# One accumulator in HBM for all routed blocks of a mixture-of-experts step: chained scatters, skipped filler rows, asserted registers

## The chip, the core and the metric

The kernel runs on one core of a Trainium2 chip. The metric is the device time of one launch in microseconds (us), as the median of several executions. Engines are called as in the profile: PE is TensorE (PEld its weight loads), DVE VectorE, ACT ScalarE, POOL GpSimd, SP SyncE. SP issues most loads and stores, POOL the indirect ones.

## The reference

One layer of a hybrid backbone on 1152 tokens (1024 + 128) of width 1024: a mixer, a residual with layer norm, a mixture of experts and a last residual with layer norm. The change lies in the mixture and in the last norm:

```python
scores = jax.nn.sigmoid((x @ p["w_router"]).astype(jnp.float32))
...
y = (jax.nn.silu(xb @ p["w_exp_gate"][e]) * (xb @ p["w_exp_up"][e])) @ p["w_exp_down"][e]
y_assign = y_blocks.reshape(-1, d)[dest] * w_sorted[:, None]
routed = jax.ops.segment_sum(y_assign, tok, num_segments=t).astype(x.dtype)
shared = (jax.nn.silu(x @ p["w_sh_gate"]) * (x @ p["w_sh_up"])) @ p["w_sh_down"]
return (routed + shared).reshape(bsz, n, d)
...
x = layer_norm(DEEPNORM_ALPHA * x + g2 * moe(h, p), p["ln2_g"], p["ln2_b"])
```

Each token goes to 8 of 64 experts, so there are 1152 x 8 = 9216 assignments. An expert's tokens are cut into blocks of 128, and the last block of an expert is filled up with filler rows.

## The kernel before

The kernel works in three phases; the change touches the third (`phase3_*`), which each engine writes out as its own program, with semaphores between them.

**Tokens and blocks.** Tokens are nine tiles of 128. The shared expert runs on them as blocks b = 0 to 8, the routed blocks follow as b = 9 + j. The number of routed blocks is known only at run time. `routed_steps` therefore loops over pairs of blocks with branches on a loaded register, and each engine reads the numbers it needs (the block count, the expert of block j, whether block j starts a new expert) with `entry`, a load of a table entry into a register (line 440).

**A step.** In step s the engines do, each in its own order:
- PE: gate and up products of block s, transpose of h of block s-1, transpose of the gathered rows of block s+2 (line 911), down product of block s-2 (lines 856 for all products).
- ACT: silu of s, high parts of h and x, the high part of a new expert's gate and up weights (line 653), the scaled copy of y of block s-2 from PSUM into one of two buffers `yb` (line 734), the high part of new down weights (line 658).
- DVE: the gate product of s, low parts, the index column of the gather (line 1157), the low part of new gate and up weights (line 987), the index column of the scatter of block s-2 (line 1162).
- POOL: the gather of block s+4 (line 614), the low part of new down weights (line 595, a 4.6 us operation), then the scatter of block s-2 (line 623).
- SP: the weight loads, 3 MB for each expert, into two buffers each, every load behind the landing of an earlier one and the splitting of the one whose buffer it takes (lines 469 to 501).

**Accumulation.** There are two accumulators in HBM, `acc_dram[0]` and `acc_dram[1]`, one for each parity p of a block. The scatter of block j is an indirect DMA that adds its 128 rows of `yb[p]` to `acc_dram[p]`. It waits for the landing of the scatter of block j-2, which is the earlier one into the same accumulator and the same buffer; the ACT copy and the DVE index copy wait for the same landing. Filler rows carry token numbers from T on and land in 128 rows behind the tokens (`NTRASH`). The shared expert's output is written plainly into `acc_dram[0]` (line 726), and `acc_dram[1]` is filled with zeros by POOL in phase 3's first lines (578 and 580), 5 MB. The gather already drops filler rows (`bounds_check=T - 1`), the scatter doesn't.

**Last stage.** When the last scatter has landed SP loads, for every tile, both accumulators and x1 (lines 563 to 566; three tiles of x1 are there already). DVE adds the two parts of tile 0 (line 1254), PE adds them for tiles 1 to 8 by products with the identity into PSUM (line 974), and DVE does the rest: times g2 (1258), plus x1 (1260), mean (1075) and normalization (1262, 1266), with ACT's square and root between.

Of the kernel before, what the change touches and what calls it, by code (L numbers as in the profile page):

```python
# [6 lines left out]
F32 = mybir.dt.float32  # L7
# [8 lines left out]
P = 128  # L16
D = 1024
# [18 lines left out]
NTRASH = P  # L36
# [78 lines left out]
def build(nc, A, out_prompt, out_sample, out_state, stage=9, dbg=None):  # L115

    ctx = ExitStack()
    with ctx:
# [9 lines left out]
        acc_dram = [nc.dram_tensor(f"acc{p}_dram", [T + NTRASH, D], F32).ap() for p in range(2)]  # L128
# [240 lines left out]
        def table(w, dtype=F32, parts=P):  # L369
# [26 lines left out]
        acc_t, acc1_t = carve(R01, GU_AT, NT, D), carve(R01, GU_AT + (NT + 1) * D, NT, D)  # L396
# [9 lines left out]
        (sel_ready, rank_mm, nb_ready, end_mm, cmp_ready, blk_mm, tables_ready, dest_ready, empty_out) = (sem(n) for n in (  # L406
             "sel_ready", "rank_mm", "nb_ready", "end_mm", "cmp_ready", "blk_mm", "tables_ready", "dest_ready",
             "empty_out"))
# [3 lines left out]
        gidx_ready, sidx_ready, sum_mm, sum_used = (sem(n) for n in ("gidx_ready", "sidx_ready", "sum_mm", "sum_used"))  # L412
# [25 lines left out]
        def entry(eng, place, min_val, max_val):  # L438

            return nc.values_load(place, engines=(eng.engine,), min_val=min_val, max_val=max_val,  # L440
                                  skip_runtime_bounds_check_because="block counts and expert numbers are bounded by the shapes")
# [18 lines left out]
        def landed_before(j, p):  # L460

            return 8 * (j - (p + 1) % 2) + 16

# [17 lines left out]
        def phase3_sync(sp):  # L481
# [21 lines left out]
            for i in range(NT + 2):  # L503
# [9 lines left out]
                if i == 2:  # L513
                    sp.wait_ge(setup_in, STATE_OUT)
                    for p in range(2):
                        sp.wait_ge(y_out[p], 16)
                    sp.wait_ge(empty_out, 16)
                    load_gate_up(sp, 0, A["w_sh_gate"][0], A["w_sh_up"][0])
                    load_down(sp, 0, A["w_sh_down"][0])
# [42 lines left out]
            for i in range(NT):  # L562
                sp.dma_start(acc_t[:, i, :], acc_dram[0][tile(i), :]).then_inc(fin_in[i], 16)
                sp.dma_start(acc1_t[:, i, :], acc_dram[1][tile(i), :]).then_inc(fin_in[i], 16)
                if i >= XE:
                    sp.dma_start(x1_t[i], x1_dram[tile(i), :]).then_inc(fin_in[i], 16)
# [7 lines left out]
        def phase3_pool(pool):  # L574
            tt = pool.tensor_tensor

            zero = S[:, SR].rearrange("p a b -> p (a b)")
            pool.dma_start(acc_dram[0][T:T + NTRASH].rearrange("p (h x) -> p h x", h=2),
                           zero.unsqueeze(1).to_broadcast((P, 2, 512))).then_inc(y_out[0], 16)
            pool.dma_start(acc_dram[1].rearrange("(p a) (h x) -> p (a h) x", p=P, h=2),  # L580
                           zero.unsqueeze(1).to_broadcast((P, 2 * (T + NTRASH) // P, 512))).then_inc(y_out[1], 16)
            pool.wait_ge(empty_out, 16)
# [34 lines left out]
            def scatter(b, p, j):  # L617

                pool.wait_ge(y_ready, b + 1)
                pool.wait_ge(sidx_ready, j + 1)  # L620
                pool.wait_ge(y_out[p], landed_before(j, p))
                pool.sem_inc(dma_turns)
                pool.indirect_dma_start(out=acc_dram[p], out_offset=bass.IndirectOffsetOnAxis(  # L623
                    ap=sidx[:, p:p + 1], axis=0), in_=yb[:, p, :], in_offset=None, compute_op=ALU.add).then_inc(y_out[p], 16)
# [20 lines left out]
        def phase3_act(act):  # L645
# [73 lines left out]
            def shared_out(b, p):  # L719
# [6 lines left out]
                act.dma_start(acc_dram[0][tile(b), :], yb[:, p, :]).then_inc(ysh_out[p], 16)  # L726
# [74 lines left out]
        def phase3_pe(pe, project):  # L801
# [165 lines left out]

            for i in range(1, NT):
                pe.wait_ge(fin_in[i], 48 if i < ST else 64)
                if i >= 3:  # L970
                    pe.wait_ge(sum_used, i - 1)
                for h in range(2):
                    for n, part in enumerate((acc_t, acc1_t)):
                        last = mm(ps[:, 2 * (i % 2) + h, :], ident, part[:, i, h * 512:(h + 1) * 512], start=(n == 0), stop=(n == 1))
                last.then_inc(sum_mm, 1)

        def phase3_dve(dve, done):
# [268 lines left out]
            for s in range(NT + 1):  # L1246
                i = s
                if i < NT:
                    x, y = acc_t[:, i, :], acc1_t[:, i, :]
                    k = 2 * NT + i  # L1250
                    r = k % 2
                    if i == 0:
                        dve.wait_ge(fin_in[0], 48)
                        done(tt(x, x, y, ALU.add))
                    else:
                        dve.wait_ge(sum_mm, i)
                    total = two(x) if i == 0 else ps[:, 2 * (i % 2):2 * (i % 2) + 2, :]
                    tt(two(x), total, two(g2_row[cond_of(i)]), ALU.mult).then_inc(sum_used, 1)
# [5 lines left out]
                if i >= 0:  # L1264
                    scale = ln_scale(2 * NT + i)
                    stt(acc_t[:, i, :], acc1_t[:, i, :], scale, ln2_row[:, 1, :], ALU.mult, ALU.add).then_inc(fin_ready, 1)
# [57 lines left out]
        def _(pool):  # L1324
# [40 lines left out]
            for r in range(2):  # L1365
                for d in range(2):
# [8 lines left out]
            pool.dma_start(list_dram.rearrange("(q c r) w -> q c (r w)", q=117, r=P),  # L1375
                           C["emptylist"][0:117].unsqueeze(1).to_broadcast((117, NE * T // P // 117, 2 * P))).then_inc(empty_out, 16)
# [812 lines left out]
```

## Time and profile before

| what | value |
|---|---|
| device time, median of 3 executions | 1862.57 us (1859.29, 1862.57, 1863.57) |
| profiled execution: span from first to last instruction | 1837.1 us |
| device time over the span, taken from the median | 25.5 us |
| PE busy, share of the span | 1708.8 us, 93% |
| mean granted TensorE clock | 0.965 |
| DMA | 102447 packets, 406.50 MB |
| first gather to landing of the last scatter, about | 709 to 1774 us |

The profiled execution's own time is its span of 1837.1 us with what lies before the first and behind the last instruction; only the span is on the page, and the median stands 25.5 us above it. Shares of busy time are averages over very different stages: what a change of the routed stage is worth has to be read in that stage.

### The profile page before, as it was taken

What the parts mean: (1) busy time and instruction counts of PE and PEld (TensorE: products, weight loads), DVE (VectorE), ACT (ScalarE), POOL (GpSimd) and SP (SyncE); (2) the same over time, 40 slices, a digit from 0 to 9 for tenths busy, and PEclk for the clock granted to TensorE, in tenths of its full rate; (3) what the DMA queues carried; (4) which work ended last, traced back from release to release, by engine and by line L of the source; (5) the groups of instructions that cost most, each with busy time, mean ns of one, the idle gap of its engine ahead of it and who ended that gap; (6) DMA issues with size and microseconds to landing.
All of it is one profiled execution on the core that took longest, in us unless ns stands there. A gap on an engine that the chain in (4) does not pass through costs nothing.

```text
span 1837.1 us, 30736 instructions
## 1 busy us (share of the span) xinstructions
PE 1708.8 (93%) x8570; PEld 1334.1 (73%) x8571; DVE 927.2 (50%) x1442; ACT 840.2 (46%) x950; POOL 759.4 (41%) x445
## 2 busy tenths in 40 slices
PE   6999999999999898999999989999999989999845
PEld 2677788888455686888877878888888768888621
DVE  7432210167578873654554455335645645456429
ACT  2320011341033433765666566445666666567612
POOL 3230000400003562665465566634774565546630
PEclk9999999999999898999999999999999999999868
DMA  8515531022542453898799899768998999889786
GB/s 347 183 50 178 169 108 33 19 93 81 194 182 89 144 182 147 281 336 267 223 303 303 256 308 351 222 180 240 328 316 234 298 303 319 237 271 319 241 257 255
DMA packets 102447, 406.50 MB, mean 221 GB/s; under 512 B 17820, under 2 KB 34457, under 8 KB 74624
## 3 DMA queue, kind: packets, MB, share of 16 engines
q1 hardware_dynamic: 62576, 289.25, 42.3%
q0 software_dynamic: 37232, 107.16, 24.0%
q10 hardware_dynamic: 2592, 9.44, 1.7%
q8 instruction: 32, 0.52, 0.1%
q14 instruction: 15, 0.12, 0.0%
HBM read 339.94 MB, written 84.72 MB: 231 GB/s over the span
## 4 chain that ended last, share of the span: by engine, by line
PE 66%; DMA 15%; DVE 8%; ACT 4%; issue 4%; POOL 2%; ACTq 1%; SPq 1%; POOLq 0%; DVEq 0%
PE ps L856 35%; PE ps L2001 12%; DMA raw<-w_exp_up 6%; DMA arena<-hx_dram,arena 5%; PE ps L911 4%; PE ps L2142 4%; PE ps L1924 2%; DMA acc_dram<-arena 2%; PE ps L2132 1%; POOL d_split L595 1%; PE ps L888 1%; PE ps L1974 1%; PE ps L2097 1%; ACT d_split L658 1%; PE ps L2036 1%
## 5 line engine op out<-in xcount | busy, mean ns | idle before, releaser
L856 PE MATMUL ps<-gu_split,xT 128*128 (+1 forms) x2712 | 637.7, 391 | 0.2 <-issue 0.2
L856 PEld LDWEIGHTS ps<-gu_split,xT 128*128 128x128 f32 x2712 | 511.3, 189 | 107.7 <-issue 0.9
L856 PE MATMUL ps<-d_split,hTe 128*128 (+1 forms) x1356 | 357.6, 415 | 34.7 <-ACT arena L734 34.6
L595 POOL TENSOR_TENSOR d_split<-raw,d_split (+1 forms) x65 | 299.5, 4608 | 194.3 <-ACT d_split L658 193.9
L987 DVE TENSOR_TENSOR gu_split<-raw,gu_split (+1 forms) x130 | 293.3, 2297 | 127.3 <-ACT gu_split L653 127.3
L856 PEld LDWEIGHTS ps<-d_split,hTe 128*128 128x128 f32 x1356 | 259.1, 197 | 90.2 <-issue 38.3
L653 ACT ACTIVATE gu_split<-raw (+1 forms) x130 | 241.2, 1907 | 62.7 <-SPq L497 61.0
L614 POOL DMA_INDIRECT arena<-hx_dram,arena x108 | 140.7, 1303 | 189.4 <-DVE arena L1157 157.5
L1151 DVE TENSOR_TENSOR arena<-ps,arena 128x256 f32<-128x256 f32 x113 | 70.5, 624 | 288.1 <-ACT arena L740 288.0
L623 POOL DMA_INDIRECT acc_dram<-arena x104 | 167.1, 1607 | 90.2 <-DVE arena L1162 60.6
L1141 DVE TENSOR_TENSOR xT<-ps,xT 128x1024 fp32r<-128x1024 f32 x115 | 140.7, 1224 | 101.0 <-ACT xT L712 101.0
L2001 PE MATMUL ps<-hT_split,w_split 128*128 128x512 f32 (+1 forms) x816 | 189.9, 390 | 0.0
L2001 PEld LDWEIGHTS ps<-hT_split,w_split 128*128 128x128 f32 x816 | 150.2, 188 | 37.1 <-issue 7.1
L734 ACT ACTIVATE arena<-ps,arena 128x1024 f32<-128x1024 f32 x104 | 115.3, 1109 | 114.4 <-PE ps L856 57.4
L712 ACT ACTIVATE xT<-ps 128x1024 fp32r<-128x1024 f32 x115 | 118.1, 1027 | 65.6 <-PE ps L911 65.2
L911 PE MATMUL ps<-const,arena 128*128 128x128 f32 x920 | 123.2, 278 | 23.0 <-DMA arena<-hx_dram,arena 15.0
L740 ACT ACTIVATE arena<-ps 128x256 f32<-128x256 f32 x113 | 43.0, 380 | 216.0 <-PE ps L856 215.9
L589 POOL DMA_INDIRECT list_dram<-arena x72 | 79.3, 1101 | 144.6 <-DVE arena L1064 123.6
L2142 PE MATMUL ps<-arena 128*128 128x512 f32 x288 | 129.6, 605 | 1.4 <-DVE arena L1092 0.8
L658 ACT ACTIVATE d_split<-raw (+1 forms) x65 | 124.1, 1909 | 7.0 <-SPq L501 4.9
L911 PEld LDWEIGHTS ps<-const,arena 128*128 128x128 f32 x920 | 106.3, 143 | 25.4 <-issue 10.0
L2142 PEld LDWEIGHTS ps<-arena 128*128 128x128 f32 x288 | 54.6, 194 | 65.2 <-issue 62.8
(284 smaller groups left out, 1433.0 us busy)
## 6 DMA issues: line engine op xcount, KB each, us to landing
raw<-w_exp_gate SPq DMA_DIRECT2D x64, 1024.0 KB
raw<-w_exp_up SPq DMA_DIRECT2D x64, 1024.0 KB
raw<-w_exp_down SPq DMA_DIRECT2D x64, 1024.0 KB
arena<-w_ada SPq DMA_DIRECT2D x16, 1024.0 KB, 4.9
arena<-x_dram SPq DMA_DIRECT2D x18, 512.0 KB, 10.7
arena<-acc_dram SPq DMA_DIRECT2D x18, 512.0 KB, 11.3
arena<-ada_halves SPq DMA_DIRECT2D x4, 2048.0 KB, 24.3
w_raw<-w_in SPq DMA_DIRECT2D x16, 512.0 KB, 4.8
```

What stands on the lines that cost most here:

```text
L595: tt(d_split(q, 1), raw_d(q), d_split(q, 0).bitcast(F32), ALU.subtract).then_inc(d_low, 1)
L614: pool.indirect_dma_start(out=xg[:, p, :], out_offset=None, in_=hx_dram, in_offset=bass.IndirectOffsetOnAxis(ap=gidx[:, p:p + 1], axis=0), ...
L623: pool.indirect_dma_start(out=acc_dram[p], out_offset=bass.IndirectOffsetOnAxis(ap=sidx[:, p:p + 1], axis=0), in_=yb[:, p, :], in_offset=N ...
L653: a(gu_split(q, 0, half * (GU // 2), GU // 2), raw_gu(q, half), ACT.Copy).then_inc(gu_high, 1)
L658: a(d_split(q, 0), raw_d(q), ACT.Copy).then_inc(d_high, 1)
L712: a(xT[:, p, 0, :].rearrange("p (h x) -> p h x", h=2), ps[:, 0:2, :], ACT.Copy).then_inc(xT_high, 1)
L856: last = mm(dst, lhs(a, j), rhs(b, j), start=(t == 0), stop=(t == len(terms) - 1))
L911: last = pe.transpose(ps[:, c // 4, (c % 4) * P:(c % 4 + 1) * P], xg[:, p, c * P:(c + 1) * P], ident)
L987: last = tt(part(1), raw_gu(q, half), part(0).bitcast(F32), ALU.subtract)
L1141: tt(two(xT[:, p, 1, :]), ps[:, 0:2, :], two(xT[:, p, 0, :].bitcast(F32)), ALU.subtract).then_inc(xT_ready, 1)
L2001: last = mm(dst, lhsT, rhs, start=(t == 0), stop=(t == len(terms) - 1))
L2142: last = mm(ps[:, 2 * (i % 2) + h, :], yT[:, j, tile(i)], w_out[:, j, h * 512:(h + 1) * 512], start=(start and j == chunks[0]), stop=(j == 1))
```

## The change

- One accumulator `acc_dram` of exactly T rows in place of two of T + 128. Nothing is filled with zeros any more, since the shared expert's plain writes cover all rows.
- The scatter of block j waits for the landing of the scatter of block j-1 (`other_landed`). ACT's and DVE's waits on the landing of block j-2 stay.
- The scatter gets `bounds_check=T - 1, oob_is_err=False`: filler rows are skipped.
- The last stage loads one accumulator for each tile. The sums of line 974 on PE and of line 1254 on DVE are gone, and DVE multiplies from SBUF.
- `entry` no longer skips the bounds check of the loaded value: behind each load stands an assertion.
- The list tensor in HBM is initialized by two DMAs in place of one, and these now bring the semaphores `y_out` to 16, in place of the two fills.

```diff
-        acc_dram = [nc.dram_tensor(f"acc{p}_dram", [T + NTRASH, D], F32).ap() for p in range(2)]
+        acc_dram = nc.dram_tensor("acc_dram", [T, D], F32).ap()
...
-            return nc.values_load(place, engines=(eng.engine,), min_val=min_val, max_val=max_val,
-                                  skip_runtime_bounds_check_because="block counts and expert numbers are bounded by the shapes")
+            return nc.values_load(place, engines=(eng.engine,), min_val=min_val, max_val=max_val)
...
+        def other_landed(j, p):
+
+            return 8 * j + 16 if p else 8 * j + 24
...
-                sp.dma_start(acc_t[:, i, :], acc_dram[0][tile(i), :]).then_inc(fin_in[i], 16)
-                sp.dma_start(acc1_t[:, i, :], acc_dram[1][tile(i), :]).then_inc(fin_in[i], 16)
+                sp.dma_start(acc_t[:, i, :], acc_dram[tile(i), :]).then_inc(fin_in[i], 16)
...
-            zero = S[:, SR].rearrange("p a b -> p (a b)")
-            pool.dma_start(acc_dram[0][T:T + NTRASH].rearrange("p (h x) -> p h x", h=2),
-                           zero.unsqueeze(1).to_broadcast((P, 2, 512))).then_inc(y_out[0], 16)
-            pool.dma_start(acc_dram[1].rearrange("(p a) (h x) -> p (a h) x", p=P, h=2),
-                           zero.unsqueeze(1).to_broadcast((P, 2 * (T + NTRASH) // P, 512))).then_inc(y_out[1], 16)
-            pool.wait_ge(empty_out, 16)
+            for p in range(2):
+                pool.wait_ge(y_out[p], 16)
...
-                pool.wait_ge(y_out[p], landed_before(j, p))
+                pool.wait_ge(y_out[1 - p], other_landed(j, p))
                 pool.sem_inc(dma_turns)
-                pool.indirect_dma_start(out=acc_dram[p], out_offset=bass.IndirectOffsetOnAxis(
-                    ap=sidx[:, p:p + 1], axis=0), in_=yb[:, p, :], in_offset=None, compute_op=ALU.add).then_inc(y_out[p], 16)
+                pool.indirect_dma_start(out=acc_dram, out_offset=bass.IndirectOffsetOnAxis(
+                    ap=sidx[:, p:p + 1], axis=0), in_=yb[:, p, :], in_offset=None, bounds_check=T - 1, oob_is_err=False,
+                    compute_op=ALU.add).then_inc(y_out[p], 16)
...
-            for i in range(1, NT):
-                pe.wait_ge(fin_in[i], 48 if i < ST else 64)
-                if i >= 3:
-                    pe.wait_ge(sum_used, i - 1)
-                for h in range(2):
-                    for n, part in enumerate((acc_t, acc1_t)):
-                        last = mm(ps[:, 2 * (i % 2) + h, :], ident, part[:, i, h * 512:(h + 1) * 512], start=(n == 0), stop=(n == 1))
-                last.then_inc(sum_mm, 1)
...
-                    if i == 0:
-                        dve.wait_ge(fin_in[0], 48)
-                        done(tt(x, x, y, ALU.add))
-                    else:
-                        dve.wait_ge(sum_mm, i)
-                    total = two(x) if i == 0 else ps[:, 2 * (i % 2):2 * (i % 2) + 2, :]
-                    tt(two(x), total, two(g2_row[cond_of(i)]), ALU.mult).then_inc(sum_used, 1)
+                    dve.wait_ge(fin_in[i], 32 if i < ST else 48)
+                    tt(x, x, g2_row[cond_of(i)], ALU.mult).then_inc(sum_used, 1)
...
-            pool.dma_start(list_dram.rearrange("(q c r) w -> q c (r w)", q=117, r=P),
-                           C["emptylist"][0:117].unsqueeze(1).to_broadcast((117, NE * T // P // 117, 2 * P))).then_inc(empty_out, 16)
+            lists = list_dram.rearrange("(q c r) w -> q c (r w)", q=117, r=P)
+            for p, (c0, c1) in enumerate(((0, 2), (2, NE * T // P // 117))):
+                pool.dma_start(lists[:, c0:c1], C["emptylist"][0:117].unsqueeze(1).to_broadcast((117, c1 - c0, 2 * P))).then_inc(y_out[p], 16)
```

Two places as they stand in the built programs. First POOL's queue in the loop over pairs, the scatter of an even j and the gather of the next block; before:

```order
L620 REGISTER_ALU [waits y_ready]
L621 ISA [waits sidx_ready]
L623 DMA acc_dram<-arena 1280x1024 [waits y_out1]
L611 REGISTER_ALU
L612 REGISTER_ALU [waits gidx_ready]
L614 DMA arena<-hx_dram,arena 128x1024 [waits x_t]
L440 ISA
L440 TENSOR_LOAD arena
L478 COMPARE_AND_BRANCH
```

and with the change (line 618 is the scatter, 609 the gather, 438 the load of a table entry):

```order
L615 REGISTER_ALU [waits y_ready]
L616 ISA [waits sidx_ready]
L618 DMA acc_dram<-arena 1152x1024 [waits y_out0]
L606 REGISTER_ALU
L607 REGISTER_ALU [waits gidx_ready]
L609 DMA arena<-hx_dram,arena 128x1024 [waits x_t]
L438 ISA
L438 TENSOR_LOAD arena
L438 ISA x2
L479 COMPARE_AND_BRANCH
```

The order is the same. The scatter of an even block waits on the other semaphore, and the next gather stands behind it as before. Behind the load stand two more instructions, of which one only computes a register and the other is the assertion.

Second the first tiles of the last stage on DVE; before (line 1254 is the sum of tile 0, 1258 the product with g2):

```order
L1254 TENSOR_TENSOR arena<-arena 128x1024 [waits fin_in0,row_ready]
L1258 TENSOR_TENSOR arena<-arena 128x1024 [waits dve_step]
L1260 SCALAR_TENSOR_TENSOR arena,small<-arena 128x1024 [waits sum_used]
L1075 TENSOR_SCALAR small<-small 128x1 [waits dve_step]
L1262 SCALAR_TENSOR_TENSOR arena<-arena,small 128x1024 [waits mean_ready]
L1258 TENSOR_TENSOR arena<-ps,arena 128x1024 [waits sum_mm,dve_step]
```

and with the change (line 1240 is the product):

```order
L1240 TENSOR_TENSOR arena<-arena 128x1024 [waits fin_in0,row_ready]
L1242 SCALAR_TENSOR_TENSOR arena,small<-arena 128x1024 [waits sum_used]
L1062 TENSOR_SCALAR small<-small 128x1 [waits dve_step]
L1244 SCALAR_TENSOR_TENSOR arena<-arena,small 128x1024 [waits mean_ready]
L1240 TENSOR_TENSOR arena<-arena 128x1024 [waits fin_in1,dve_step]
```

The sum of tile 0 is gone, and tile 1 waits for its own load in place of PE's sum.

## Rows read from the trace of the kernel before

**Rows 1.** The page's head: busy us (share of the span) x instructions.

```profile
span 1837.1 us, 30736 instructions
PE 1708.8 (93%) x8570; PEld 1334.1 (73%) x8571; DVE 927.2 (50%) x1442; ACT 840.2 (46%) x950; POOL 759.4 (41%) x445
```

**Rows 2.** Stretches of the routed stage: length, engines' busy us, clock, DMA share, GB/s.

```profile
1110.00:1290.00 180.00, 180.00 (x894) 151.16 (x894) 81.16 (x115) 96.39 (x103) 90.42 (x47) 1.00 0.82 245
...
1290.00:1370.00 80.00, 77.64 (x385) 64.94 (x384) 42.62 (x53) 52.15 (x50) 57.00 (x23) 1.00 0.96 331
1450.00:1520.00 70.00, 59.03 (x266) 48.17 (x265) 35.94 (x41) 44.59 (x41) 42.48 (x18) 0.93 0.95 306
1690.00:1770.00 80.00, 59.33 (x248) 47.12 (x246) 29.64 (x37) 41.58 (x38) 46.55 (x21) 0.86 0.82 241
```

**Rows 3.** Who waited for whom: us in total, times, longest.

```profile
PE ps L856 <- ACT arena L734: 34.6, 12, 6.3
PE ps L911 <- DMA arena<-hx_dram,arena: 15.0, 8, 7.1
...
ACT arena L734 <- DMA acc_dram<-arena: 57.0, 22, 6.3
```

**Rows 4.** The scatter's line: ns of its issue on POOL min/median/max; its landing.

```profile
L623 POOL DMA_INDIRECT acc_dram<-arena x104: 1557/1589/3474, 761.4 to 1767.8; - x104
...
DMA to landing us min/median/max: 5.8/10.8/13.5
```

**Rows 5.** DMA queue of POOL: packets, MB, share of 16 engines' span.

```profile
q0 software_dynamic: 37232, 107.16, 24.0%
```

**Rows 6.** POOL in order of time, 1331 to 1356: start us, us, what [idle before].

```profile
1332.81 1.59 POOL L623 DMA_INDIRECT acc_dram<-arena  x1 [0.16 <-issue]
1334.71 1.03 POOL L614 DMA_INDIRECT arena<-hx_dram,arena  x1 [0.31 <-issue]
...
1340.57 1.59 POOL L623 DMA_INDIRECT acc_dram<-arena  x1 [0.17 <-issue]
1342.46 2.32 POOL L614 DMA_INDIRECT arena<-hx_dram,arena  x1 [0.30 <-issue]
```

**Rows 7.** PE in order of time, 1343 to 1360: the transposes of gathered rows.

```profile
1348.13 1.09 PE L911 MATMUL ps<-const,arena 128*128 128x128 f32 x8 [1.52 <-DMA arena<-hx_dram,arena]
...
1357.51 1.04 PE L911 MATMUL ps<-const,arena 128*128 128x128 f32 x8
```

**Rows 8.** POOL in order of time, 1744 to 1775: the last three scatters.

```profile
1756.85 1.59 POOL L623 DMA_INDIRECT acc_dram<-arena  x1 [0.17 <-issue]
1761.84 1.56 POOL L623 DMA_INDIRECT acc_dram<-arena  x1 [3.40 <-ACT arena L734]
1767.83 1.56 POOL L623 DMA_INDIRECT acc_dram<-arena  x1 [4.43 <-ACT arena L734]
```

**Rows 9.** The chain that ended last, 1747 to 1774: start us, us, what.

```profile
1747.69 11.91 DMA acc_dram<-arena
...
1767.83 6.13 DMA acc_dram<-arena
1774.13 0.32 SPq L563
```

**Rows 10.** DVE in order of time, 1774 to 1791: the first tiles of the last stage.

```profile
1779.10 1.23 DVE L1254 TENSOR_TENSOR arena<-arena 128x1024 f32<-128x1024 f32 x1 [13.65 <-DMA arena<-acc_dram]
...
1783.07 1.28 DVE L1262 SCALAR_TENSOR_TENSOR arena<-arena,small 128x1024 f32<-128x1024 f32 x1
1789.12 1.23 DVE L1258 TENSOR_TENSOR arena<-ps,arena 128x1024 f32<-128x1024 f32 x1 [4.77 <-PE ps L974]
```

**Rows 11.** Line 563, the loads of the first accumulator: issue to landing.

```profile
DMA to landing us min/median/max: 3.7/10.9/15.6
```

**Rows 12.** Line 440, a register operation beside PE's table loads, ns min/median/max.

```profile
L440 PEldq FUSED_REGOPS  x206: 46/46/57, 741.3 to 1751.2; - x103
```

**Rows 13.** Who POOL waited for: us in total, times, longest.

```profile
POOL list_dram L589 <- DVE arena L1064: 123.6, 3, 108.3
```

More of the change, by code:

```diff
@@ L35 @@
 PAIRS = (NB + 1) // 2
-NTRASH = P
 GU = 2 * D * FF // P
@@ L395, in build @@
         ln2_row = carve(R0, 6 * D, 2, D)
-        acc_t, acc1_t = carve(R01, GU_AT, NT, D), carve(R01, GU_AT + (NT + 1) * D, NT, D)
+        acc_t, norm_t = carve(R01, GU_AT, NT, D), carve(R01, GU_AT + (NT + 1) * D, NT, D)
         g2_row = [carve(R0, 8 * D, D), carve(R01, GU_AT + NT * D, D)]
@@ L405, in build @@
         x0r_in, x1_out, h2_out = (x0r_in0, x0r_in1), (x1_out0, x1_out1), (h2_out0, h2_out1)
-        (sel_ready, rank_mm, nb_ready, end_mm, cmp_ready, blk_mm, tables_ready, dest_ready, empty_out) = (sem(n) for n in (
-             "sel_ready", "rank_mm", "nb_ready", "end_mm", "cmp_ready", "blk_mm", "tables_ready", "dest_ready",
-             "empty_out"))
+        (sel_ready, rank_mm, nb_ready, end_mm, cmp_ready, blk_mm, tables_ready, dest_ready) = (sem(n) for n in (
+             "sel_ready", "rank_mm", "nb_ready", "end_mm", "cmp_ready", "blk_mm", "tables_ready", "dest_ready"))
         list_out, logit_out, list_row_ready, list_in, list_t, lists_ready = (sem(n) for n in (
@@ L411, in build @@
         mean_ready, sq_ready, std_ready = sem("mean_ready"), sem("sq_ready"), sem("std_ready")
-        gidx_ready, sidx_ready, sum_mm, sum_used = (sem(n) for n in ("gidx_ready", "sidx_ready", "sum_mm", "sum_used"))
+        gidx_ready, sidx_ready, sum_used = (sem(n) for n in ("gidx_ready", "sidx_ready", "sum_used"))
         dma_turns = sem("dma_turns")
@@ L516, in phase3_sync @@
                         sp.wait_ge(y_out[p], 16)
-                    sp.wait_ge(empty_out, 16)
                     load_gate_up(sp, 0, A["w_sh_gate"][0], A["w_sh_up"][0])
@@ L725, in shared_out @@
                 act.wait_ge(y_ready, b + 1)
-                act.dma_start(acc_dram[0][tile(b), :], yb[:, p, :]).then_inc(ysh_out[p], 16)
+                act.dma_start(acc_dram[tile(b), :], yb[:, p, :]).then_inc(ysh_out[p], 16)
             def routed_out(b, p, j):
@@ L1248, in phase3_dve @@
                 if i < NT:
-                    x, y = acc_t[:, i, :], acc1_t[:, i, :]
+                    x, y = acc_t[:, i, :], norm_t[:, i, :]
                     k = 2 * NT + i
                     r = k % 2
-                    if i == 0:
-                        dve.wait_ge(fin_in[0], 48)
-                        done(tt(x, x, y, ALU.add))
-                    else:
-                        dve.wait_ge(sum_mm, i)
-                    total = two(x) if i == 0 else ps[:, 2 * (i % 2):2 * (i % 2) + 2, :]
-                    tt(two(x), total, two(g2_row[cond_of(i)]), ALU.mult).then_inc(sum_used, 1)
+                    dve.wait_ge(fin_in[i], 32 if i < ST else 48)
+                    tt(x, x, g2_row[cond_of(i)], ALU.mult).then_inc(sum_used, 1)
                     dve.wait_ge(sum_used, i + 1)
@@ L1265, in phase3_dve @@
                     scale = ln_scale(2 * NT + i)
-                    stt(acc_t[:, i, :], acc1_t[:, i, :], scale, ln2_row[:, 1, :], ALU.mult, ALU.add).then_inc(fin_ready, 1)
+                    stt(acc_t[:, i, :], norm_t[:, i, :], scale, ln2_row[:, 1, :], ALU.mult, ALU.add).then_inc(fin_ready, 1)
         @block.sync
```

## The prediction, as written before the changed kernel ran

> **What bounds the kernel now.** I began with the page's head: PE is busy in 93% of a span of 1837.1 us [rows 1], so whatever leaves PE's program full costs nothing. The reader should see that this is an average. I then cut the routed stage, 1110 to 1770, into stretches [rows 2]. From 1110 to 1290 PE is busy in all 180 us, at full clock, with the DMA engines at 0.82: that stretch is bound by PE's instructions. In the three others shown PE is idle for 2.4, 11.0 and 20.7 us, 34 us in all, with DMA shares of 0.96, 0.95 and 0.82. These are the places where experts with a single block follow each other, so that every step needs another 3 MB of weights. Third I read who waited for whom [rows 3]: PE's products wait 34.6 us for ACT's copy of y, its transposes 15.0 us for gathers, and ACT's copy waits 57.0 us for landings of scatters, mostly without PE noticing. Fourth the scatter itself [rows 4]: 104 of them in 1006 us, one every 9.8 us, and a landing of 10.8 us in the median, 5.8 at least. That is the danger of this change: a chain of scatters, each behind the landing of the last, would need 10.8 us for each block if the median held, and there are 9.8.
>
> **The change part by part.** The sum is made against the profiled execution, whose time I take as 25.5 us above its span, which is the median of 1862.57 us.
>
> *The last stage* is the surest part. DVE starts at 1779.10, when both parts of tile 0 have landed, adds them, ends tile 0's work at 1784.35 and then stands for 4.77 us until PE has summed tile 1 [rows 10]. From 1789.12 on it works without a gap, and keeps doing so. With one accumulator tile 0 needs only its first load, issued at 1774.13 [rows 9] and landed 3.7 us later in the best case [rows 11]: start at 1777.9, 1.2 us earlier. The sum of tile 0 goes, 1.25 us from start to start. The wait of 4.77 us goes as well, since tile 1 needs only its own load, the next in the queue, and DVE has some 4 us of work on tile 0. Together -7.2 us. The product with g2 costs the same from SBUF as from PSUM: the two additions and products shown all take 1.23 us. What is late next is DVE itself, over nine tiles. Ends of the range: -5 us if the load takes a median-like time, -8 if it is as fast as it can be.
>
> *The drain* in front of it gets longer. The last four scatters are issued at 1747.69, 1756.85, 1761.84 and 1767.83; the first lands after 11.91 us, at 1759.60, the last, alone on the queue, after 6.13 us [rows 8, 9]. Chained, with 6.1 us for each and 0.2 us from a landing to the next issue: the second is issued at 1759.8 and lands at 1765.9, the third 1766.1 and 1772.2, the fourth 1772.4 and 1778.5, where it was 1773.96. That is +4.5 us; with the least landing of 5.8 us [rows 4] +3.6, with the median for one of them +9. I take +4.5, as 6.13 is the row of a lone scatter in this very place. The Trainium skill (DMA: Bandwidth & Descriptors, section Anatomy of one DMA) fits such a transfer as about 2.0 us plus bytes over 436 GB/s. That gives some 3.2 us for the 512 KB here, the chain would then be ready before the fourth block is, the drain would cost nothing and the sum would be 4.5 us lower. The trace has no scatter under 5.8 us, so the measurement decides.
>
> *The chain in the middle.* Where scatters are far apart, the one ahead has landed. Where two are 5 to 8 us apart, the second now waits. But they share one queue: the second also landed late before, up to 13.5 us after its issue [rows 4], as its rows stood behind those of the first. Its landing hardly moves, and ACT's and DVE's waits are for landings. POOL waits in the second scatter, and behind it stand only the next gather and the next low part. I take 0 for the waits: POOL is busy for 41% of the span [rows 1] and has idle time in front of most gathers. Bounds: nothing, and 20 us (second rival).
>
> *The skipped rows.* Of 104 x 128 = 13312 rows 9216 are assignments, 4096 (31%) filler. POOL's queue moves 107.16 MB in 24.0% of the span of all engines [rows 5]; the scatters carry 54.5 MB of it. By bytes that is half, 224 us, 2.2 us of all sixteen engines for one scatter. So 31% is 69 us of transfer time, but in PE-bound stretches nobody waits for it. It can only pay in the 34 us of idle time. Ends: 0 and -34. I take -2, near the lower end, for two reasons. The largest loss, 20.7 us of 80, is where the DMA share is lowest, 0.82 [rows 2]: a chain of single waits (load, split on ACT, DVE and POOL, next load), not the mean traffic. And filler rows are always the tail of a block. A load ends with its slowest engine, and rows taken from the tail relieve it only if the rows of a scatter are dealt to the engines in turn. The Trainium skill (same page, section The descriptor swizzle) says that they are not: partitions 0 to 63 belong to engines 0 to 7, so a block of 40 to 64 tokens leaves eight engines empty and gives the others all their eight rows. By it the relief is near 0; with rows dealt evenly it would be ten times what I take (first rival). No row here separates the engines.
>
> *The assertions.* Each table load gets two more register instructions behind it. The nearest row is a fused register operation of 46 ns, 206 of them on PE [rows 12], so 2 x 206 x 0.046 = 19 us of PE's sequencer. In the 180 us without a gap the loads of both blocks of each step are already hidden behind queued matmuls, and 0.1 us each stays hidden too. I take 0 (ends: 0 and +19).
>
> *The fills and the list.* The 5 MB of zeros went out long before they were needed: POOL stands 123.6 us in front of its list scatters, waiting for DVE [rows 13]. If that cover were gone, two issues on POOL would count, about 2 us. The list's second DMA is hidden by the same wait. Nine loads fewer on SP are in the last stage's term. All 0.
>
> **Sum:** -7.2 + 4.5 - 2 = -4.7 us, so 1857.9 us.
>
> **Rivals.**
> 1. *The skip relieves the loads.* If rows are dealt evenly, about 21 blocks in the three stretches lose a third to a half of 2.2 us, 14 to 23 us; I price it at 20. For it: shares of 0.95 and 0.96 with PE idle [rows 2]. Against it: what stands above. Time: 1862.6 - 2.7 - 20 = 1839.9.
> 2. *The gather behind the waiting scatter* (slower). Scatters at 1332.81 and 1340.57, a gather at 1342.46 [rows 6]. With a landing of 11.4 us the second now waits until 1344.2, 3.7 us, and pushes that gather to 1346.2. The gather ahead of it, issued at 1334.71, held PE up for 1.52 us at 1348.13, so it took 13.3 us; the next is needed at 1357.51 [rows 7]. From 1346.2 that makes 1359.5: PE stands 2.0 us. There are ten places with scatters some 7.8 us apart, so +20 us, 1877.9. It decides where a delay is over the gather's slack, here 1.7 us. Against it: the gather's 13.3 us held its time behind the scatter's rows in the queue, which now have left earlier.
> 3. *The assertions show* on PE or ACT: up to +19 us, 1877.
> 4. *The skip skips nothing* that costs, because the filler rows' descriptors are still made and moved: the sum loses its 2 us, 1859.9. The gather has the same check and takes 1.03 us on POOL where the scatter takes 1.59 [rows 6], which speaks against more cost there.
>
> **How the numbers follow.** My forecast has 0.54, rivals 1 to 4 have 0.16, 0.14, 0.07 and 0.09. About 0.2% of the time, 3.7 us, is what a measurement of this kernel can tell from no change. Faster by more than that means under 1858.8: a little over half of the forecast (its own range is 1853 to 1864, from the ends of the first two terms and a few us of relief or stall), and all of rival 1, 0.48. Within 0.2%: a third of the forecast, most of rival 4, some of 2 and 3, 0.29. Slower: the rest, 0.23. The range from 1841 to 1871 takes in the forecast, rival 4, half of rival 1 and the milder forms of rivals 2 and 3.
>
> **What would show it.** Right: line 974 is gone, DVE goes from tile 0 to tile 1 without a gap and the stretch from SP's first load to the end is some 56 us long, not 63; the last scatter is issued at the landing of the third, about 6 us before SP's first load; POOL's queue has 4096 packets and 17 MB less; PE is still busy in the whole of a stretch of multi-block experts. Wrong: a sum of PE waits for gathers clearly over 15.0 us (rival 2), a DMA share that falls in the bad stretches together with PE's idle time (rival 1), gaps on PE or ACT behind table loads (rival 3), an unchanged packet count (rival 4).

## The result, and the profile of the changed kernel

| | before | changed |
|---|---|---|
| device time, median | 1863.07 us (4 executions) | 1901.58 us (1893.56 to 1906.46, 4 executions) |
| ratio of the times, 95% interval | | 1.021 (1.0183 to 1.0237) |
| profiled execution: span | 1837.1 us | 1891.8 us |

The changed kernel is slower by 38.5 us. I had forecast 1857.9 us, in a range that ended at 1871, so the forecast is wrong in sign and in size.

First, from the changed kernel's page, the head and the queue of POOL; under them who waited for whom (us in total, times, longest). They answer to [rows 1, 3, 5]:

```profile
span 1891.8 us, 32015 instructions
PE 1689.9 (89%) x8506; PEld 1322.7 (70%) x8507; DVE 930.9 (49%) x1441; ACT 845.2 (45%) x950; POOL 776.8 (41%) x444
...
q0 software_dynamic: 35808, 84.65, 18.8%
```

```profile
POOL acc_dram L618 <- DMA acc_dram<-arena: 212.9, 43, 8.9
...
ACT arena L730 <- DMA acc_dram<-arena: 90.1, 30, 7.1
...
PE ps L907 <- DMA arena<-hx_dram,arena: 34.2, 17, 8.0
...
PE ps L852 <- ACT arena L730: 32.1, 11, 7.0
```

The queue has lost 22.5 MB: 16.7 MB of filler rows and 5.8 MB of fills. It has lost only 1424 packets, and all of them before the routed stage; why the filler rows' 4096 packets are still there is shown below. PE's idle time hasn't fallen but grown. Its products still wait as long for ACT's copies as before, 32.1 us, but its transposes now wait 34.2 us for gathers, where they waited 15.0 [rows 3]. POOL has a wait that it never had: 212.9 us for landings of scatters, in 43 places. My second rival describes both.

Now one place in order of time, POOL and then PE (start us, us, line, and in brackets the idle time ahead and what ended it):

```profile
1128.66 3.22 POOL L618 DMA_INDIRECT acc_dram<-arena  x1 [2.59 <-DMA acc_dram<-arena]
1132.19 1.05 POOL L609 DMA_INDIRECT arena<-hx_dram,arena  x1 [0.30 <-issue]
...
1138.55 2.96 POOL L618 DMA_INDIRECT acc_dram<-arena  x1 [0.64 <-issue]
1141.82 1.37 POOL L609 DMA_INDIRECT arena<-hx_dram,arena  x1 [0.31 <-issue]
1150.15 1.60 POOL L618 DMA_INDIRECT acc_dram<-arena  x1 [6.97 <-DVE arena L1149]
1152.06 1.04 POOL L609 DMA_INDIRECT arena<-hx_dram,arena  x1 [0.30 <-issue]
```

```profile
1150.82 0.38 PE L884 MATMUL ps<-const,arena 128*128 128x128 f32 x2
1153.08 1.09 PE L907 MATMUL ps<-const,arena 128*128 128x128 f32 x8 [1.88 <-DMA arena<-hx_dram,arena]
```

The gathers leave right behind the scatters, at 1132.19, 1141.82 and 1152.06: 9.6 and 10.2 us apart, and PE's step is 9.3. PE's transposes at 1153.08 need the gather of 1141.82, which left behind the scatter of 1138.55 and took 10.7 us; by then POOL had already stood 2.59 us for the landing that the scatter of 1128.66 waited for. PE stands for 1.88 us, and the delay stays. The scatter of 1138.55 lands at 1149.2; the next may not leave before, and goes at 1150.15. The row puts POOL's idle 6.97 us down to DVE's index copy of 1149.3, but that copy is the next scatter's, and had waited for the same landing.

The chain of work that ended last shows the pace. Its longest pieces between 1093 and 1120 (start us, us, what) are landings in a row:

```profile
1093.62 10.90 DMA acc_dram<-arena
...
1105.56 10.54 DMA acc_dram<-arena
...
1118.43 9.36 DMA acc_dram<-arena
```

From scatter to scatter it takes 11.9 and 12.9 us here, against the step of 9.3. Of the whole span's chain 12% are landings of scatters, where it was 2%. Where PE isn't late it loses nothing. From 1180 to 1340 it is busy all the time, as in [rows 2]:

```profile
1180.00:1340.00 160.00, 160.00 (x792) 134.33 (x792) 66.93 (x97) 85.58 (x89) 79.25 (x40) 1.00 0.71 208
```

The loss comes in jumps of 1 to 6 us where single-block experts bring weight loads beside the scatters, and little of it is made good.

The drain and the last stage answer to [rows 8 to 11]. The chain that ended last, then DVE in order of time, then the accumulator's loads:

```profile
1804.71 10.76 DMA acc_dram<-arena
...
1816.34 5.84 DMA acc_dram<-arena
...
1823.05 5.95 DMA acc_dram<-arena
...
1829.83 6.22 DMA acc_dram<-arena
...
1836.22 3.49 DMA arena<-acc_dram
```

```profile
1839.80 1.22 DVE L1240 TENSOR_TENSOR arena<-arena 128x1024 f32<-128x1024 f32 x1 [17.33 <-DMA arena<-acc_dram]
...
1842.52 1.28 DVE L1244 SCALAR_TENSOR_TENSOR arena<-arena,small 128x1024 f32<-128x1024 f32 x1
1843.83 1.22 DVE L1240 TENSOR_TENSOR arena<-arena 128x1024 f32<-128x1024 f32 x1
```

The last four scatters go one behind the other, 11.6, 6.7 and 6.8 us apart. From SP's first load to the end it is 1891.8 - 1836.2 = 55.6 us, where it was 63.0, and DVE goes from tile 0 to tile 1 without a gap.

**The two spans can't be subtracted.** The changed kernel's profiled execution took 1893.56 us by its own clock, 1.8 over its span. By the same 1.8 the profiled execution of before took 1838.9, which is 20 us under the fastest of its timed ones. Aligned by PE's shared-expert and routed steps, the two traces are level (within 0.5 us) until 655 us and 22.2 us apart at the first routed step, before any routed scatter. The time goes at two places, 660 to 670 and 685 to 700, where the profile shows nothing that PE waits for and its matmuls still come one by one, as here:

```profile
661.74 0.19 PE L810 MATMUL ps<-arena 128*128 128x64 bf16 x1 [1.24 <-issue]
663.14 0.21 PE L810 MATMUL ps<-arena 128*128 128x64 bf16 x1 [1.21 <-issue]
665.23 0.21 PE L810 MATMUL ps<-arena 128*128 128x64 bf16 x1 [1.89 <-issue]
667.34 0.21 PE L810 MATMUL ps<-arena 128*128 128x64 bf16 x1 [1.89 <-issue]
```

Whether the change brought this was one of the questions for the runs.

### The profile page after: what moved, and what is told of

It reads as the page before. It is cut to its first block, busy times and chain, and to the rows that moved or that the text cites. A ratio compares the mean times of both kernels' runs of the same rounds, so it can differ in the third digit from the quotient of the medians.

```text
span 1891.8 us, 32015 instructions
## 1 busy us (share of the span) xinstructions
PE 1689.9 (89%) x8506; PEld 1322.7 (70%) x8507; DVE 930.9 (49%) x1441; ACT 845.2 (45%) x950; POOL 776.8 (41%) x444
## 4 chain that ended last, share of the span: by engine, by line
PE 55%; DMA 19%; DVE 8%; issue 7%; POOL 4%; ACT 4%; POOLq 1%; ACTq 1%; SPq 0%; DVEq 0%
PE ps L852 27%; DMA acc_dram<-arena 12%; PE ps L1984 11%; DMA arena<-hx_dram,arena 4%; PE ps L2125 4%; PE ps L907 3%; POOL d_split L590 3%; DMA raw<-w_exp_up 3%; PE ps L1907 2%; PE ps L2115 1%; PE ps L1957 1%; ACT gu_split L649 1%; ACT d_split L654 1%; PE ps L884 1%; PE ps L2019 1%
## 5 line engine op out<-in xcount | busy, mean ns | idle before, releaser
L852 PE MATMUL ps<-d_split,hTe 128*128 (+1 forms) x1356 | 358.2, 415 | 38.0 <-ACT arena L730 32.1
L974 DVE TENSOR_TENSOR gu_split<-raw,gu_split (+1 forms) x130 | 297.3, 2328 | 142.2 <-ACT gu_split L649 141.1
L618 POOL DMA_INDIRECT acc_dram<-arena x104 | 190.1, 1828 | 310.6 <-DMA acc_dram<-arena 212.9
L609 POOL DMA_INDIRECT arena<-hx_dram,arena x108 | 135.7, 1257 | 87.7 <-DVE arena L1144 52.6
L907 PE MATMUL ps<-const,arena 128*128 128x128 f32 x920 | 126.1, 282 | 42.2 <-DMA arena<-hx_dram,arena 34.2
L736 ACT ACTIVATE arena<-ps 128x256 f32<-128x256 f32 x113 | 42.9, 380 | 190.4 <-PE ps L852 184.6
L2125 PEld LDWEIGHTS ps<-arena 128*128 128x128 f32 x288 | 53.5, 190 | 65.4 <-issue 61.2
```

The costliest lines, as they stand in the source:

```text
L609: pool.indirect_dma_start(out=xg[:, p, :], out_offset=None, in_=hx_dram, in_offset=bass.IndirectOffsetOnAxis(ap=gidx[:, p:p + 1], axis=0), ...
L618: pool.indirect_dma_start(out=acc_dram, out_offset=bass.IndirectOffsetOnAxis(ap=sidx[:, p:p + 1], axis=0), in_=yb[:, p, :], in_offset=None ...
L852: last = mm(dst, lhs(a, j), rhs(b, j), start=(t == 0), stop=(t == len(terms) - 1))
L907: last = pe.transpose(ps[:, c // 4, (c % 4) * P:(c % 4 + 1) * P], xg[:, p, c * P:(c + 1) * P], ident)
L974: last = tt(part(1), raw_gu(q, half), part(0).bitcast(F32), ALU.subtract)
L2125: last = mm(ps[:, 2 * (i % 2) + h, :], yT[:, j, tile(i)], w_out[:, j, h * 512:(h + 1) * 512], start=(start and j == chunks[0]), stop=(j == 1))
```

## The experiments

Ratios are to the kernel before, timed beside each run on the same chip, with their 95% intervals. 0.001 is 1.9 us. In free_empty and wait_empty a part of the computation is left out.

| run | accumulators | wait | skip | registers | median us | ratio |
|---|---|---|---|---|---|---|
| assert_only | 2 | no | no | asserted | 1865.8 | 1.0028 (1.0011 to 1.0046) |
| clamp_two | 2 | no | no | clamped | 1859.4 | 0.9991 (0.9975 to 1.0007) |
| skip_two_acc | 2 | no | yes | asserted | 1861.0 | 1.0003 (0.9984 to 1.0022) |
| wait_two_acc | 2 | yes | no | asserted | 1912.0 | 1.0258 (1.0217 to 1.0299) |
| wait_half | 2 | every second | no | asserted | 1890.8 | 1.0176 (1.0146 to 1.0206) |
| one_acc_no_skip | 1 | yes | no | asserted | 1906.0 | 1.0248 (1.0222 to 1.0274) |
| clamp_one_acc | 1 | yes | yes | clamped | 1892.3 | 1.0184 (1.0156 to 1.0212) |
| gather_first | 1 | yes, a step later | yes | asserted | 1962.6 | 1.0552 (1.0523 to 1.0582) |
| free_empty | 2 | no | all rows | asserted | 1831.9 | 0.9856 (0.9830 to 0.9883) |
| wait_empty | 2 | yes | all rows | asserted | 1834.2 | 0.9863 (0.9838 to 0.9888) |
| clamp_skip_two | 2 | no | yes | clamped | 1855.3 | 0.9973 (0.9957 to 0.9988) |
| lean_two | 2 | no | yes | clamped | 1856.0 | 0.9981 (0.9963 to 1.0000) |

**The parts alone.** In assert_only only the reason that let the assertions be left out is taken from the kernel before:

```diff
-            return nc.values_load(place, ..., skip_runtime_bounds_check_because="...")
+            return nc.values_load(place, engines=(eng.engine,), min_val=min_val, max_val=max_val)
```

> The kernel before with the assertions of the loaded registers alone; two accumulators, no new wait, no skip. Theory W (the loss is the wait of a scatter for the landing of the one ahead, with the gathers behind it on POOL): the PE step is 9.3 us and its sequencer runs ahead, so the assertions show at most in the unprotected stretches: 1860 to 1868. Theory A (the loss is the assertions: two register operations and a check, about 0.2 us at each load of the expert tables on every engine): 1890 to 1905, with PE idle behind the table loads. Theory C (part of the loss, up to 22 us, is the two places between 660 and 700 us where PE's matmuls come 1.2 to 1.9 us apart with nothing to wait for, which the new code brought): only a profile that has them here would blame the assertions' code.

Measured: +5 us by the ratio (2 to 9). The median, 1865.8, lies in the range of theory W and far from that of theory A. In clamp_two one register operation takes the place of each assertion:

```diff
...
+            with eng.register() as r:
+                eng.reg_alu(r, v, min_val, mybir.AluOpType.max)
+                return eng.snap(r, min_val=min_val, max_val=max_val)
```

> The kernel before, where each loaded register is held above its least value by one register operation instead of the two and the check of an assertion; nothing else. Theory W: within 4 us of the kernel before, 1860 to 1866. Theory A: a third to a half of the loss, 1873 to 1885. Theory C: no slow matmuls at 660 to 700 us if the kernel before has none either; if they are here too, they belong to every kernel's executions and explain nothing of the difference.

Measured: level with before. So the assertions cost 5 to 7 us, and the rows of the changed kernel's table loads show what I had priced at 0.1 us for each load (ns min/median/max):

```profile
L438 PEldq FUSED_REGOPS  x416: 46/151/170, 745.7 to 1806.9; - x139
...
L438 PEldq SEQ_ASSERT  x210: 18/18/26, 745.9 to 1807.1; - x105
```

The row mixes two kinds: 206 operations still take 0.046 us [rows 12], and the 210 added ones take 0.16. With the assertion that is 0.18 us for each load. Both runs also answer for the slow matmuls. The profiles of all twelve runs have them at the same two places. They cost 18 to 22 us over the profile of before (20 in clamp_two, 22 in the changed kernel), and the timed executions of before are as long as if they had them. So they are most likely no part of the difference.

wait_two_acc adds the new wait to assert_only, and skip_two_acc the skip:

```diff
-                pool.wait_ge(y_out[p], landed_before(j, p))
+                pool.wait_ge(y_out[1 - p], other_landed(j, p))
```

> The kernel before with the assertions and with the new wait (each scatter for the landing of the one ahead of it), still two accumulators, filler rows still written. Theory W: the loss of about 35 us in the routed stage comes back whole and the 7 us that the last stage gained don't, so 1900 to 1915, with PE waiting 30 us or more for gathers. Theory A: the same as with the assertions alone.

> The kernel before with the assertions and the skipped filler rows; two accumulators, no new wait. Theory W: the same as with the assertions alone or up to 5 us less, 1856 to 1866; the software queue moves 17 MB less. Theory that the skip relieves the weight loads (my first rival): 14 to 23 us less than with the assertions alone.

Measured: the wait costs (1.0258 - 1.0028) x 1862 = 43 us by itself (35 to 51 by the two intervals), more than the whole result; the time is in the range of theory W. Of it 5 us are the drain, from PE's last product to the last landing, which is 13.8 us long in the profile of wait_two_acc and 8.6 in that of assert_only. The skip gives about 5 us back, hardly more than the two intervals leave open, and not the 14 to 23 of my first rival. The packets of assert_only and then of skip_two_acc:

```profile
DMA packets 102447, 406.50 MB, mean 218 GB/s; under 512 B 17820, under 2 KB 34457, under 8 KB 74624
```

```profile
DMA packets 102447, 389.75 MB, mean 209 GB/s; under 512 B 21916, under 2 KB 38553, under 8 KB 74624
```

A skipped row saves its bytes and not its packet: 4096 packets of 4096 bytes have become 4096 packets of 8 bytes.

Who waited in wait_two_acc between PE's first and last routed step, then the same in assert_only:

```profile
PE ps L859 <- ACT arena L737: 27.4, 12, 4.5
PE ps L914 <- DMA arena<-hx_dram,arena: 23.6, 18, 3.1
PE ps L859 <- issue: 5.6, 10, 1.0
PE ps L914 <- issue: 3.6, 1, 3.6
```

```profile
PE ps L855 <- ACT arena L733: 22.8, 10, 4.0
PE ps L910 <- DMA arena<-hx_dram,arena: 12.0, 9, 3.0
PE ps L855 <- issue: 2.1, 5, 0.5
```

The same steps take 42.9 us more; with the drain the two profiled executions are 48.1 us apart. PE's waits for gathers hold 11.6 us of it, those for copies 4.6, the remaining waits (the two issue rows, and 2.1 us for hTe) 9.2. The rest is PE itself, busy for 999.7 us instead of 982.5 with the same matmuls. The granted clock over the stretch is 0.97 where it was 0.98: its records stand at 1.2 GHz in place of 2.4 for 61 us in wait_two_acc and for 31 us in assert_only. In the changed kernel it is 0.80 from 1158 to 1166, right behind the gap shown above. But there the two levels hardly explain PE's longer work: 37.5 us at 1.2 GHz in its routed stage, where it was 34.1 before, with PE busy for 988.9 us and not 977.8. What the rest of that is stays open.

**Is it the order on POOL, or the length of the landings?** gather_first issues each scatter a step later, behind that step's gather:

```diff
                 gather(s + 4, p, j + 4)
...
+                scatter(s - 3, 1 - p, j - 3)
                 if_new(pool, j, down_low)
...
-                scatter(s - 2, p, j - 2)
...
```

The conditions that keep the first blocks right, and the one scatter more behind the loop, are left out here.

> The changed kernel with another order on POOL: each scatter is issued one step later, right behind the gather of that step and ahead of the low part, so that the scatter ahead of it has had a whole step of 9.3 us to land and no gather stands long behind a scatter's wait. Theory G (the loss comes to PE through gathers that wait behind scatters): PE's waits for gathers fall from 34 us to under 20, POOL's waits for landings from 213 us to under 100, and the time to 1875 to 1890. Theory L (the chain of landings is itself longer than a step, so that the wait only changes its place): POOL's waits move to ACT's copies and PE's products, and the time stays at 1895 to 1910.

Measured: PE no longer waits for a routed gather, and the kernel is slower still, by 61 us of the medians and 64 by the ratios. Who waited in it:

```profile
ACT arena L734 <- DMA acc_dram<-arena: 312.5, 63, 12.0
...
POOL acc_dram L618 <- DMA acc_dram<-arena: 163.2, 43, 9.4
...
PE ps L856 <- ACT arena L734: 111.4, 44, 6.3
```

The wait has moved to ACT's copies, which need the buffer of y that the late scatter still reads. Theory L is nearer, but it too had no such loss: with two gather buffers and two of y, an order that spares one makes the other late.

wait_empty and free_empty leave every row but the first token's out of the scatters, with the wait and without:

```diff
-                    ... in_=yb[:, p, :], in_offset=None, compute_op=ALU.add)
+                    ... in_=yb[:, p, :], in_offset=None, bounds_check=0, oob_is_err=False, compute_op=ALU.add)
```

> Two accumulators, assertions, and the full wait of each scatter for the landing of the one ahead, but every row beyond the first token's is left out of the scatters, so that the experts' results are not added (that part of the computation is missing). Chain theory: landings fall to 2 to 3 us, the chain has 3 to 4 us in a step of 9.3, and the wait costs 0 to 5 us against the same without the wait. Theory of order (what costs is the waiting instruction in front of POOL's gathers and low parts, whatever it waits for): 20 us or more remain.

> The same without the new wait: two accumulators, assertions, the scatters' rows left out (that part of the computation is missing). It is what wait_empty is compared with, and it shows what the traffic of 107 MB of accumulated rows costs the rest: if the weight loads are bound by the DMA engines in the stretches of single blocks, 1830 to 1850; if the traffic is hidden, 1858 to 1866.

Measured: 1.3 us apart by the ratios, 2.3 by the medians, both within the intervals. POOL still waits for landings in wait_empty:

```profile
POOL acc_dram L626 <- DMA acc_dram<-arena: 102.9, 27, 5.9
```

That is 102.9 us of waits in front of gathers and low parts, and they cost next to nothing. The longest is 5.9 us, less than a step; in wait_two_acc, with the rows in, POOL waits 219.1 us for landings and 10.4 at the longest. So waits on POOL have no price of their own here. Leaving the rows out did two things at once, though. It made the landings short, and it let the gathers land some 3 us further ahead of PE's steps in the middle (in free_empty, against assert_only), which hides a delay. The runs don't part the two. Counted from the landing events, the middle landing is 6.2 us in wait_empty, not the 2 to 3 that I expected, and one in 104 takes over 9.3; in wait_two_acc 48 do. The scatters aren't empty: the queue still has all its 37232 packets, 13304 of them now of 8 bytes. (The expectation of free_empty calls all of the queue's 107 MB scatters. The queue fell to 52.78 MB, so the scatters are half of it.) free_empty also shows what the scatters' bytes and their longer landings cost the rest: 32 us against assert_only by the ratios, some 4 of them in the drain, and the time is in the first of its two ranges. The skip gets 5 of them because filler rows are 31% of the rows and many lie in blocks whose traffic nobody waits for; the reason is argued, not tested.

**How much of the chain does it take?** In wait_half only the scatters with p = 1 wait:

```diff
                 pool.wait_ge(y_out[p], landed_before(j, p))
+                if p:
+                    pool.wait_ge(y_out[0], other_landed(j, 1))
```

> Two accumulators, assertions, filler rows written; only every second scatter waits for the landing of the one ahead, the others as in the kernel before. The full wait cost 46 us over the kernel with the assertions alone (1865.8). Chain theory (what costs is that landing and issue of each scatter add up to 9.4 us or more in a row, against a step of 9.3; a break after each pair lets the next start at once): far less than half, 1867 to 1880. Theory of a price for each wait (0.45 us for each of 103): half, 1885 to 1892.

Measured: +28 us over assert_only, by the ratios, of the full wait's 43. My chain theory had expected 1 to 14, so it was wrong in this form. The other theory's range, 1885 to 1892, holds the 1890.8, but a price for each wait, whatever it waits for, is what wait_empty speaks against. The count of scatters issued while the one ahead is still in flight fits both: 50 in assert_only, 26 in wait_half, none in wait_two_acc; and 32 in free_empty, none in wait_empty, where the landings are short and the wait is free. So what costs, as far as these runs show, is a scatter held back behind a long landing, and it need not be part of a long chain. Half of them held back cost 28 us of 43, which is half or more within the intervals.

**With one accumulator.**

> The changed kernel without the skip: the accumulator has 128 more rows again and the filler rows are added there. So far the assertions cost 4 us, the skip with two accumulators gave 5 back, and the new wait cost 46. Chain theory (a scatter may go only when the one ahead has landed, and the landing of a short block is quicker because of the skip, 2.6 us against 6 and more): without the skip the chain is slower than the 5 us say, 1908 to 1918. Theory that the skip saves the same with and without the wait: 1905 to 1908.

> The changed kernel with one register operation in place of each assertion. Both kernels with two accumulators differ by 6 us there (1865.8 and 1859.4). If what the assertions cost adds up with the rest: 1893 to 1897. If it hides behind the waits of the chain: 1899 to 1902.

Measured: the skip is worth 7 us here (1.0248 to 1.0210) and 5 with two accumulators, too near to tell apart; the time lies in the range of the second theory. (The 2.6 us of the first theory is too short: counted from its issue, the quickest scatter of the changed kernel lands after 4.2 us.) The clamp gives 5 us here too (1.0210 to 1.0184), just under the range of "adds up" and no more than the two intervals leave open. The parts add up: 5 for the assertions, 43 for the wait, some -5 for the skip, and -2 for the single accumulator (1.0258 to 1.0248). That makes 41, and 39 were measured. The -2 is a poor measurement, with intervals that leave 9 us either way: both runs have the chained drain, and the last stage alone is 6.3 us shorter in the profile of one_acc_no_skip (55.7 us, not 62.0).

**A version that may beat both.** clamp_skip_two is the kernel before with the clamp and the skip. lean_two also drops the filler rows of the accumulators and their zeros:

```diff
+            for p, (a0, a1) in enumerate(((0, NT), (NT, 2 * NT))):
+                pool.dma_start(acc1[:, a0:a1, :], zero...).then_inc(y_out[p], 16)
```

> The kernel before (two accumulators, no new wait, no assertions) with the skipped filler rows and each loaded register held by one operation: a candidate to beat both. If the parts add up (clamp -2, skip -5 against the kernel before): 1853 to 1857. If the skip's gain was noise of that pair: 1858 to 1862.

> The candidate once more, made leaner: two accumulators of 1,152 rows, no rows for fillers and so no zeros for them, the zeros of the second accumulator in two halves, filler rows skipped, each loaded register held by one operation, no new wait. If the candidate's 1855.3 was no accident: 1852 to 1857, below the kernel before in the same call by 0.2% or more.

Measured: 0.27% and 0.19% faster than before. The first interval lies wholly under 1, the second touches it. Both medians lie in their ranges, but the 0.2% that lean_two was to show is just missed. The leaner zeros bring nothing that can be seen.

## Why the prediction was wrong, step by step

- *The last stage*, -7.2 us: right. The stretch fell from 63.0 to 55.6 us. DVE starts 3.6 us after SP's first load (before 5.0), the sum and the gap are gone. The profiles with two accumulators and full scatters have 61.2 to 63.2 us for it, so the change is worth 5.6 to 7.6.
- *The drain*, +4.5: right in kind, too small. From PE's last product to the last landing it took 8.3 us and takes 14.6, +6.3. A lone landing is 5.8 to 6.2 us as I took it, but from a landing to the next issue it is 0.8 to 0.9 us, not 0.2. The Trainium skill's fit (DMA: Bandwidth & Descriptors, section Anatomy of one DMA), 3.2 us by my estimate for such a transfer, isn't reached by any of them.
- *The chain in the middle*, 0: **this step failed.** It stood on two legs. The first, "Its landing hardly moves", was nearly right. Of the scatters of assert_only 50 were issued while the one ahead was in flight, and both of such a pair were down 18.1 us after the first's issue, in the middle. The same pairs one behind the other in wait_two_acc take 18.4; pair by pair the middle shift is +1.1 us. The second leg, "I take 0 for the waits" on POOL, was wrong. The second scatter's issue moves by 4.1 us in the middle, to 0.8 behind a landing, and what stands behind it on POOL moves too: against the steps of PE that need them, the gathers are issued 1.5 us later in the middle. My first paragraph had the comparison that warns, 10.8 us against 9.8 for each block: in wait_two_acc a scatter that leaves within 1 us of a landing goes 11.2 us after the one ahead in the middle, and PE's step is 9.3. POOL's 41% of busy time, an average over the span, said nothing about those places. The step costs some 38 us, the 43 of the wait less 5 of the drain.
- *The second rival* was the mechanism: a gather behind a waiting scatter, PE waiting for gathers. Its chance was 0.14 and its price 20 us, by ten places of 2.0 us. In the changed kernel's trace 57 of the 103 scatters after the first leave within 1 us of a landing (before, 20 do). PE waits for gathers 16 times in the routed stage, 26.2 us (before, 7 times, 7.9 us). These 18 us more are about the rival's price; the rest of the 38 us is waits for copies, small waits and PE's own longer work, none of which it named.
- *The skipped rows*, -2: right in sign; 5 to 7 us. The sign that I named for it, 4096 packets fewer, did not come. The packets are still there, as the fourth rival had it, but the skip saves time all the same. Whether the Trainium skill's swizzle (DMA: Bandwidth & Descriptors, section The descriptor swizzle) is why it saves no more stays open, as no run separates the engines. By that page's list a block of 40 tokens gives eight rows to engines 0 and 1 and four to each of the next six, not eight to all.
- *The assertions*, 0: too small. +5 to +7 us, from a register operation of 0.16 us where I counted 0.046. Still about a third of my upper end.
- *The fills and the list*, 0: lean_two shows nothing for the zeros. The list's split wasn't tried alone.
- *The base*: I took 25.5 us around the span as a constant. It is 1.8 us; most of the rest was an execution without the slow matmuls. A ratio isn't touched by that, but two spans are.

What stays open is how the cost divides between late gathers and late copies. gather_first changed both at once, and a third gather buffer, which would tell them apart, wasn't tried.

## What to carry to other kernels

Before you put a wait between two transfers that used to overlap, compare landing plus issue with the step of the engine that bounds. While it was shorter here, the wait was free even though its engine stood for 100 us in total; where it was longer, everything queued behind the waiting instruction got late with it. Look where landings are slowest, not at their mean spacing. And check that the profiled execution's own time fits the timed ones before you build a sum on its span.

## What the runs showed that I had not expected

- At two places between 655 and 700 us PE's matmuls come up to 1.9 us apart with nothing to wait for. Together they cost 18 to 22 us in each of thirteen profiles; the profile of before alone is without them. PE is busy in 50.0 of the 50 us from 650 to 700 there, in 36.0 of the changed kernel's. The Trainium skill (Runtime: NRT & Kernel Launch, section Instruction fetch mechanics) says that crossing into a new block of code is mostly hidden. The traces can't confirm or refute that here: blocks of 16 KB are fetched in assert_only at 652.7 and 682.2, near both places, but they take 1.3 and 1.7 us, and the slow matmuls go on for some 10 us each time; the profile of before has such fetches too (655.2, 675.7 and 695.1), and no slow matmuls. The cause is open. After the wait and the scatters' bytes it is the largest cost that these runs came upon.
- Adding rows in DRAM is dear even without the new wait: 32 us of 1866 for 54 MB.
- A row that the bounds check skips still costs a packet, of 8 bytes in place of 4096. Scatters with nearly all rows skipped still land after 6.2 us in the middle (wait_empty).
- Scatters that no longer overlap land a little sooner: 8.6 us in the middle in wait_two_acc, 10.8 in assert_only. Two at once are done hardly earlier than two in a row, 18.1 and 18.4 us after the first's issue. What the overlap buys is the early issue of the second, and with it the engine that issues.
